# Gate and up chunks 1 to 9 with three seven-product units instead of two, and the low parts of three plain slots made by adding transfers

## What is computed

```python
h = _rmsnorm(x, norm_g)
return (jax.nn.silu(h @ w_gate) * (h @ w_up)) @ w_down      # 2048 -> 5632 -> 2048
```

## Time and profile before

| | |
|---|---|
| runs (median of 3) | 2593.36 us (2592.0 to 2594.75) |
| span of the profiled execution | 2591.4 us, 1.96 us under the median; the profile gives no other time of that execution |
| PE busy | 2562.1 us, 99% |
| DVE, ACT, POOL busy | 1954.8 us (75%), 1339.8 us (52%), 189.2 us (7%) |
| DMA | 548.21 MB, mean 212 GB/s |

### The profile page before, as it was taken

One profiled execution on the slowest core, in us unless ns is written; L12 is line 12 of the kernel. 1 busy time (PEld: TensorE's weight loads), 2 busy tenths in 40 slices (PEclk: granted clock), 3 DMA queues, 4 the chain that ended last, 5 costly groups with the idle time before them and its releaser, 6 DMA issues.

```text
span 2591.4 us, 34224 instructions
## 1 busy us (share of the span) xinstructions
PE 2562.1 (99%) x13659; PEld 2103.4 (81%) x13659; DVE 1954.8 (75%) x2311; ACT 1339.8 (52%) x1568; POOL 189.2 (7%) x346
## 2 busy tenths in 40 slices
PE   8999999999999999999999999999999999999998
PEld 7888888888888777878788888888888888888887
DVE  6888888887767796959666766555668888888876
ACT  5555555555556366446455544433455455555554
POOL 2000000000000011010001112000100000000000
PEclk9999999999999999999999999999999999999999
DMA  6767676667776575656488779643767677766655
GB/s 213 232 210 242 210 236 218 217 208 228 216 210 195 184 228 159 179 165 181 146 280 257 252 245 281 201 155 130 239 190 230 222 226 225 227 219 218 210 201 175
DMA packets 278576, 548.21 MB, mean 212 GB/s; under 512 B 25020, under 2 KB 35424, under 8 KB 278032
## 3 DMA queue, kind: packets, MB, share of 16 engines
q1 hardware_dynamic: 253904, 478.60, 58.3%
q0 software_dynamic: 24192, 66.89, 8.8%
q10 hardware_dynamic: 320, 0.53, 0.1%
HBM read 508.15 MB, written 37.77 MB: 211 GB/s over the span
## 4 chain that ended last, share of the span: by engine, by line
PE 86%; DVE 8%; ACT 3%; DMA 2%; issue 1%; POOL 0%; SPq 0%; DVEq 0%; ACTq 0%; POOLq 0%
PE pp L794 14%; PE pp L795 14%; PE pp L796 14%; PE pp L415 11%; PE pp L416 11%; PE pp L417 11%; DVE wlo L376 2%; PE pa L794 1%; PE pb L796 1%; PE pb L795 1%; PE pb L794 1%; PE pa L795 1%; PE pa L796 1%; ACT whi L371 1%; DMA raw<-in_ffn_w_up 1%
## 5 line engine op out<-in xcount | busy, mean ns | idle before, releaser
L376 DVE TENSOR_TENSOR wlo<-raw,whi 128x1024 fp32r<-128x1024 f32 (+1 forms) x764 | 919.6, 1216 | 345.9 <-ACT whi L371 326.2
L371 ACT ACTIVATE whi<-raw 128x1024 fp32r<-128x1024 f32 (+1 forms) x764 | 798.0, 1053 | 626.5 <-PE pp L417 438.1
L794 PE MATMUL pp<-whi,xhi 128*128 128x512 f32 x1040 | 404.6, 389 | 0.0
L795 PE MATMUL pp<-whi,xlo 128*128 128x512 f32 x1040 | 404.6, 389 | 0.0
L796 PE MATMUL pp<-wlo,xhi 128*128 128x512 f32 x1040 | 404.6, 389 | 0.0
L415 PE MATMUL pp<-whi,xhi 128*128 128x512 f32 (+1 forms) x928 | 370.6, 399 | 0.7 <-DVE xlo L533 0.7
L417 PE MATMUL pp<-wlo,xhi 128*128 128x512 f32 (+1 forms) x928 | 359.6, 388 | 0.1
L416 PE MATMUL pp<-whi,xlo 128*128 128x512 f32 (+1 forms) x928 | 359.6, 387 | 0.0
L847 ACT ACTIVATE whi<-tw 128x1024 fp32r<-128x1024 f32 x124 | 131.6, 1062 | 276.3 <-PE pp L796 131.6
L794 PEld LDWEIGHTS pp<-whi,xhi 128*128 128x128 f32 x1040 | 195.2, 188 | 40.7
L796 PEld LDWEIGHTS pp<-wlo,xhi 128*128 128x128 f32 x1040 | 195.2, 188 | 40.6
(11 more groups left out here) (528 smaller groups left out, 3669.7 us busy)
## 6 DMA issues: line engine op xcount, KB each, us to landing
raw<-in_ffn_w_gate SPq DMA_DIRECT2D x176, 512.0 KB, 4.3
raw<-in_ffn_w_up SPq DMA_DIRECT2D x176, 512.0 KB, 4.7
raw<-in_ffn_w_down SPq DMA_DIRECT2D x176, 512.0 KB, 4.6
raw<-in_w_in SPq DMA_DIRECT2D x144, 512.0 KB, 4.3
hid_dram<-hid_t POOLq DMA_DIRECT2D x43, 512.0 KB, 5.0
xq<-hid_dram POOLq DMA_DIRECT2D x156, 128.0 KB, 3.8
raw<-in_w_lift SPq DMA_DIRECT2D x32, 512.0 KB, 5.9
raw<-in_w_out SPq DMA_DIRECT2D x32, 512.0 KB, 5.1
```

Of the source, the lines that this page charges most:

```text
L371: nc.scalar.activation(whi[:, s, :, 0:width], raw[:, r % RING, :, 0:width], ACT.Copy).then_inc(whi_ready, 1)
L376: nc.vector.tensor_tensor(wlo[:, s, :, 0:width], raw[:, r % RING, :, 0:width], whi[:, s, :, 0:width].bitcast(F32), ALU.subtract).then_inc( ...
L794: nc.tensor.matmul(out, a_hi, whi[:, s, block, :], start=start, stop=False)
L795: nc.tensor.matmul(out, a_lo, whi[:, s, block, :], start=False, stop=False)
```

## The change

Chunks 1 to 9 (`THREE`) of both FFNs get a third unit: slots 5, 6 and 7 of gate and up, after plain slots 1, 3 and 5. With t0 to t9 for the 10 plain slots left, the order is t0 t1 U1 t2 t3 U2 t4 t5 U3 t6 t7 t8 t9. Chunk 10 keeps two units. In chunks 1 to 9 the low parts of t0, t2 and t4 (`LO_ADDED`) no longer come from DVE: ACT writes minus the rounded weights into one of two extra buffers `alo` (`less_hi`), and a transfer issued by POOL adds the weights to it, straight from device memory (`add_raw`). PE reads its low weights there. The SiLU of chunks 1 to 9 moves behind t0 of the next chunk on ACT; `hidden_hi` comes after t8, and `hidden_lo` right behind the gate sum after t9. The forms of the activations for slot 5 are made once per FFN in chunk 0. A few semaphores are merged (`ident_ready` into `consts_ready`, `r_cumx` into `r_cum`, `r_rz` into `r_tilde`), with the same waits in other numbers. Shortened to its core:

```diff
-GU_UNITS, GU_AFTER = (6, 7), (1, 5)
+THREE = range(1, NFC - 1)
+def gu_units(i):
+    return ((5, 6, 7), (1, 3, 5)) if i in THREE else ((6, 7), (1, 5))
+LO_ADDED = (0, 2, 4)
...
+        xs_5 = at("xs_5", AR + 80, [4, P])
+        xshi_5 = at("xshi_5", AR + 36, [4, P], F32R)
+        xslo_5 = at("xslo_5", AR + 38, [4, P], F32R)
+        alo = [at(f"alo{k}", kib, [SK, CW], F32R) for k, kib in enumerate((AR + 32, AR + 76))]
...
+        def wait_lo(eng, n):
+            if n in ADDED:
+                eng.wait_ge(whi_ready, n + 1)
+                eng.wait_ge(sem(f"lo_added{ADDED[n] % 2}"), 16 * (ADDED[n] // 2 + 1))
+            else:
+                eng.wait_ge(wlo_ready, n + 1 - sum(a < n for a in ADDED))
         def raw_free(sp, r):
             if r >= RING:
-                sp.wait_ge(wlo_ready, freed_by[r - RING] + 1)
+                n = freed_by[r - RING]
+                if n in ADDED:
+                    sp.wait_ge(whi_ready, n + 1)
+                    sp.wait_ge(sem("lo_less_hi"), ADDED[n] + 1)
+                else:
+                    wait_lo(sp, n)
...
+        def less_hi(act, n):
+            r, k = raw_of[n], ADDED[n]
+            act.wait_ge(*loaded(r))
+            if k > 1:
+                act.wait_ge(slot_used, list(ADDED)[k - 2] + 1)
+            nc.scalar.activation(alo[k % 2][:, :, :], raw[:, r % RING, :, :], ACT.Copy, scale=-1.0).then_inc(sem("lo_less_hi"), 1)
+        def add_raw(pool, n, w):
+            k = ADDED[n]
+            pool.wait_ge(sem("lo_less_hi"), k + 1)
+            nc.gpsimd.dma_start(alo[k % 2][:, :, :], w.bitcast(F32R),
+                                accum_op=ALU.add).then_inc(sem(f"lo_added{k % 2}"), 16)
...
             for i in range(NFC):
-                hidden_out(pool, tag, i)
+                added = added_of(tag, i + 1)
+                for n, w in added[:2]:
+                    add_raw(pool, n, w)
+                hidden_out(pool, tag, i, lambda: [add_raw(pool, n, w) for n, w in added[2:]])
...
             hi(w + 1, whi[:, (w + 1) % RING, :, :], tw[:, 0:2, :])
+            if ahead is not None:
+                ahead()
...
                 for t, (_, _, w, _) in enumerate(pair["plain"]):
                     split_hi(act, w, 0)
-                    if t in GU_AFTER:
-                        unit_act(act, pair, GU_AFTER.index(t), (tag, "gu", i))
+                    if t == 0 and i - 1 in THREE:
+                        gate_silu(i - 1)
+                    if t in after:
+                        n = after.index(t)
+                        ahead = (lambda: less_hi(act, added[n + 1])) if n + 1 < len(added) else None
+                        unit_act(act, pair, n, (tag, "gu", i), ahead)
...
+                if i + 1 in THREE:
+                    less_hi(act, gu[2 * i + 2]["pair"]["plain"][LO_ADDED[0]][2])
...
                 for t, (_, _, w, _) in enumerate(pair["plain"]):
-                    split_lo(dve, w, 0)
+                    if w not in ADDED:
+                        split_lo(dve, w, 0)
...
-                    if t == pair["na"] + 2:
+                    if t == after[-1] + 3:
                         combine(dve, pair, cb, (tag, "gu", i))
-                    if t == pair["na"] + 3:
+                    if t == after[-1] + 4:
                         combine_last(dve, cb, (tag, "gu", i))
                         v.tensor_tensor(cb[:, 0:2, :], pair_of(gate), cb[:, 0:2, :], ALU.add).then_inc(sem(gate["released"][0]), 1)
+                        if i in THREE:
+                            hidden_lo(dve, tag, i - 1, hhi[:, 4 * i - 4:4 * i, :], hlo[:, 4 * i - 4:4 * i, :])
```

More of the change, by code:

```diff
@@ L737, in x_moved_lo, with added_of @@
             moved_lo(dve, tag, c, xhi[:, 4 * c:4 * c + 4, :], xlo[:, 4 * c:4 * c + 4, :], gain)
+        def added_of(tag, i):
+            weights = A["ffn1_w_gate" if tag == "f1" else "ffn2_w_gate"][0], A["ffn1_w_up" if tag == "f1" else "ffn2_w_up"][0]
+            pair = prods[tag + "gu"][2 * i]["pair"] if i in THREE else None
+            out = []
+            for t in LO_ADDED if i in THREE else ():
+                pr, j, n, _ = pair["plain"][t]
+                w = weights[0 if pr is pair["a"] else 1]
+                out.append((n, w[j * SK * P:(j + 1) * SK * P, i * CW:(i + 1) * CW].rearrange("(k p) n -> p k n", p=P)))
+            return out
         def hidden_turns(pool, tag):
@@ L795, in product @@
             nc.tensor.matmul(out, a_lo, whi[:, s, block, :], start=False, stop=False)
-            return nc.tensor.matmul(out, a_hi, wlo[:, s, block, :], start=False, stop=stop)
+            return nc.tensor.matmul(out, a_hi, (wlo[:, s, :, :] if lo is None else lo)[:, block, :], start=False, stop=stop)
         def plain_pe(pe, pair, t, acts, tts=range(TT), used=1):
@@ L966, in ffn_act, with gate_silu @@
                     forms_hi(act, xs_gu[:, :, :, :], xshi[:, :, :, :], (tag, "x"))
+                    forms_hi(act, xs_5[:, :, :], xshi_5[:, :, :], (tag, "x5"))
+            less_hi(act, gu[2]["pair"]["plain"][LO_ADDED[0]][2])
+            def gate_silu(i):
+                gate = gu[2 * i]
+                act.wait_ge(sem(gate["released"][0]), gate["released"][1])
+                for tt in range(TT):
+                    op = nc.scalar.activation(gs[:, tt, :], cb[:, tt, :], ACT.Silu, scale=rstd[:, tt:tt + 1])
+                op.then_inc(sem("acts_ready"), 1)
@@ L967, in ffn_act @@
             for i in SEVEN:
                 pair = gu[2 * i]["pair"]
-                gate = pair["a"]
+                after = pair["after"]
+                added = [pair["plain"][t][2] for t in LO_ADDED] if i in THREE else []
                 for t, (_, _, w, _) in enumerate(pair["plain"]):
                     split_hi(act, w, 0)
-                    if t in GU_AFTER:
-                        unit_act(act, pair, GU_AFTER.index(t), (tag, "gu", i))
-                    if t == pair["na"]:
+                    if t == 0 and i - 1 in THREE:
[4 more added lines that the diff above has]
+                        unit_act(act, pair, n, (tag, "gu", i), ahead)
+                    if t == after[-1] + 1:
@@ L975, in ffn_act @@
                         act.wait_ge(nat_ready, n0 + i)
                         copy_first(act, pair, cb[:, 0, :])
-                    if t == pair["na"] + 3:
+                    if t == after[-1] + (3 if i in THREE else 4):
+                        if i == NFC - 1:
+                            act.wait_ge(slot_used, pair["units"][-1][1] + UW)
                         hidden_hi(act, tag, i - 1, hhi[:, 4 * i - 4:4 * i, :])
[L979 to L983, removed]
+                    if t == after[-1] + 5:
+                        gate_silu(i)
@@ L2946, in _ @@
         def _(pe):
-            pe.wait_ge(ident_ready, 1)
+            pe.wait_ge(consts_ready, 1)
             gain_turn(pe)
```

98 lines of the change are left out of this document (55 added, 43 removed).

## The result

The changed kernel takes **2753.98 us** (median of 4 runs, 2752.67 to 2761.89) against 2594.06 for the kernel before, run beside it: ratio 1.062, 95% interval 1.0603 to 1.0637. It is slower by 159.9 us, where 49.7 was forecast and 2695 was the range's upper end. The direction and the loop were right; the size was not.

A forecast was written before the change was run, and what follows sets the result against it. PE bound the kernel at 42.16 us a chunk; the change's raw-buffer loop of 43.8 plus 1.3 for transfers gives 45.1. Per FFN 9 x (45.1 - 42.16) - 1.6 = 24.9, twice 49.7: 2643 us, range 2590 to 2695.

The forecast's parts named there:

- the saving: Chunks 1 to 9 of both FFNs: 21 matmuls instead of 24 per added pair, 12.2 us if PE never waits.
- the loop over the two raw places: All units and t8, t9 share two of four raw buffers, so loads wait for third lows: 43.8 us a chunk.
- the bare loop: Rival: adding transfers do not disturb the loads, +26 us, 2620 us; chance 0.25.
- signs named ahead: PE 97 or 98% busy, waiting for `wlo` before unit parts; gate sums 45 us apart; loads issued at the third low ahead.
- So I add 1.3 us a chunk, once: Delay of loads by adding transfers, t4's overlapping U3's pair: 1.3 us a chunk, making the period 45.1.
- its upper bound of 4.7: Most that adding transfers delay a chunk's loads, if each counts double and all three meet a load: 4.7 us.
- POOL's fetches beside other pairs mostly do not show: Argument for undisturbed loads: POOL's fetches mostly show no delay of raw pairs they run beside; no size given.
- t0's meets U1's up load, which has 1.8 us to spare: t0's adding transfer meets U1's up load, whose 1.8 us of slack takes up the delay.
- the add at 5 to 6 us: Each 512 KB adding transfer issued by POOL taken to last 5.0 to 6 us, like POOL's store of that size.
- PE is not in this loop: Chunk's loop of raw buffers runs without PE, which only waits at each unit's last parts.
- heavy transfers: Rival: every add meets a load at double weight, period 47.5 to 48.5, +93 us, 2686 us; chance 0.17.
- Faster: Rival: the loop does not bind, PE stays the bound at 41.48 us a chunk, 2581 us; chance 0.10.

The follow-up runs named there:

- e10: Changed kernel with raw pairs freed at a unit's second low, fetches held until U3's up load landed, all lows on DVE, no adding transfers: 2591.48 us, ratio 0.9967.
- e11: e10 with the turned unit order in gate and up units alone, the down parts' units in the old order: 2588.08 us, ratio 0.9962.
- e5: Changed kernel without adding transfers (some low parts wrong) and with POOL's four fetches held until U3's up load landed: 2622.85 us, +24.5.
- e1: Changed kernel with its 54 adding transfers left out (low parts of t0, t2, t4 wrong), all other waits and the order kept: 2657.95 us, +60.3.
- e3: Changed kernel with POOL's four fetches of hidden values held until U3's up load has landed, adding transfers kept: 2703.21 us, +105.6.
- e7: Changed kernel with raw pairs freed at a unit's second low, late fetches, adding transfers for t0 and t2 only, t4's low on DVE: 2677.73 us, ratio 1.0301.
- e9: Changed kernel with early freed raws, late fetches, `less_hi` one place earlier on ACT, an adding transfer for t2 only: 2620.63 us, ratio 1.0084.
- e2: Changed kernel with plain copies instead of adds in the 54 transfers, so t0, t2 and t4 hold raw weights as low parts: 2709.74 us, +112.1.

## Why the prediction was right or wrong

**Right: the bound before, and the saving.** PE was the bound, and 18 pairs in units save 12.2 us only where PE never waits. e10 and e11 show a chunk of 41.5; they gain 7.5 and 8.8 us by their own medians, not all 12.2. Not every chunk is that short: the mean of e10's sixteen distances is 41.72, against 42.15 in the kernel before, and 18 x 0.43 = 7.7 is about what e10 gains. Why single chunks take up to 42.6 was not tried. The down parts hardly change the sum: in e10 the first FFN's takes 238.2 us instead of 234.0, the second's 231.8 instead of 233.7.

**Right: the loop over the two raw places.** 43.8 us by its rows of the trace of before, 43.87 in the chunk of e5 shown, and +24.5 us where the bare loop was to give +26. (By the mean of 44.05 it would be some +31; the difference is within what single runs differ by, so part of this closeness may be luck.) U1's 7.89, the unit's 5.30 and the way from U3 to the next gate sum held within 0.1 us in both chunks shown. Most signs named ahead came too, though PE's share fell to 95%, not to 97 or 98: PE waits for `wlo` ahead of unit parts (the first of the two largest entries of PE's waits over the run, below), and the loads go out at the third low ahead. DVE's work fitted, as counted.

```profile
PE pa L860 <- DVE wlo L934: 58.8, 41, 3.9
PE pp L860 <- DMA alo<-in_ffn_w_gate: 51.5, 33, 3.9
```

**Wrong: "So I add 1.3 us a chunk, once", and its upper bound of 4.7.** The mean period is 51.41, so the term is 51.41 - 43.8 = 7.6. Some 5.3 of it lie at U3's pair (a mean of 10.5 us to the first sum against 5.2), 1.4 at U1's up load (6.2 against 4.8), 0.9 ahead of U2's first sum, and 0.2 within U1. I priced a load's meeting with *one* transfer, by the distance of two loads that are issued together. At U3's pair three things meet: t4's add, the four fetches and the loads behind the pair. e1 and e3 take one of them away each, and it needs both to bring the pair back to 5.2. The bound was wrong for the same reason: it counted transfers and left out the fetches. Without the fetches it holds: from e5 to e3 the mean distance grows by 48.30 - 44.05 = 4.25.

**Wrong: "POOL's fetches beside other pairs mostly do not show".** I put that down for the bare loop. The unit whose pair the fetches met had slack before; in the loop, each such microsecond is paid. e1 against e5 prices them at 35.8 us. The pair at 291.54, which landed late with those fetches under way, was the row to go by, and I left it out of the sum.

**Wrong in part: "t0's meets U1's up load, which has 1.8 us to spare".** It met it, and used more than that up: DVE waits 2.10 us for it in the chunk shown, and in e1 and e5 the wait is gone (4.72 to the first sum). "t2's is nearly over when U2's pair goes out" held: that pair landed after 4.0 and 4.9 us here, 4.1 and 5.0 in the mean.

**Wrong for t0: the add at 5 to 6 us, and t4's as "the shortest of time".** t4's transfers land after 6.0 us in the median, close to the forecast, and PE waits 19.2 us for them over the run. t0's land after 8.1 (8.4 in the chunk shown), and PE waits 32.3 us for them; the prediction gave t0's transfer no wait of PE at all. In the change most of these 51.5 us lie beside the loop, which is longer: in e3 PE waits 59.1 us for transfers, and the time is 54 us less. But "PE is not in this loop" fails in three of the sixteen chunks: PE's wait for t0's transfer holds back the third high part of U1 on ACT, and U1 takes up to 9.87 us. How much of the waits the end of the kernel sees was not tried alone. In e7 and e9 PE is in the chain, and there they count.

**The rule on adds.** A load of 512 KB takes 54.0% x 2752.3 / 478.6 MB x 0.524 MB = 1.63 us of the 16 DMA engines; an add takes (14.8% x 2752.3 - 8.6% x 2656.2) / 54 = 3.3 us, the 8.6% being the same queue in e1; a plain copy from POOL, worked out the same way from e2, 2.0 us. So an add takes 2.0 times a load, and 1.6 times a plain copy from the same queue. The Trainium skill, in Collectives: The Full Stack, section The bandwidth ceiling, says of a collective's reduce step that its add needs two source reads and so reaches half the rate of a copying step. Against a load these runs agree, against a plain copy from POOL they show less. By that rule alone the forecast would have been 2666, still 88 us short. What the add costs this kernel beyond a plain copy is e2's 47.8 us; the rest is who meets whom.

**The rivals.** The measured time is past heavy transfers (2686), the nearest of them; it has the add at double weight but not the fetches. (Its periods of 47.5 to 48.5 come to 2686 to 2704, so the range's end at 2695 left out half of it, not a third.) The bare loop is what e5 shows, without transfers. Faster needs a shorter loop, and e10 is that.

## What to carry to other kernels

Before a change to an order, list which loads share a place in a small ring, and add up the loop from load to load; a page on which every engine has room says nothing about it. Work moved to DMA was not free here: look at what is issued within some 6 us of each load of the loop (an add took 6.1 to land), small fetches too, and price the meeting of all of them at once, by the bytes that move before the load has landed. Freeing a buffer earlier, by turning two steps of its user, made the third unit pay here, together with later fetches; sparing a busy engine that still met its times did not.

## What the runs showed of the hardware

Transfers in company slow each other far more than the mean share tells: in the chunk shown U3's pair landed 7.3 and 10.8 us after the third low, where e5 has 3.9 and 5.2 in the median, in a stage with a mean DMA share of 0.75. While the pair was under way the share was 1.03, and what grew was the bytes moved in that time, not the time per byte: by the means of sixteen chunks 2.57 MB in 10.4 us, against 1.31 MB in 5.3 us in e5.

A wait of PE can cost more than its length. Timeline and busy times of the changed kernel around PE's wait for t0's transfer (the columns of the windows are those of the earlier trace rows):

```profile
321.67 0.47 PE L860 MATMUL pp<-whi,xhi 128*128 128x512 f32 x1 [2.79 <-DMA alo<-in_ffn_w_gate]
...
322.58 0.63 PE L860 MATMUL pp<-whi,xhi 128*128 128x512 f32 x1
...
323.86 0.63 PE L860 MATMUL pp<-whi,xhi 128*128 128x512 f32 x1
```

```profile
314.50:318.50 4.00, 4.00 (x20) 3.29 (x18) 2.78 (x3) 2.75 (x4) 0.00 (x0) 1.00 0.87 180
321.70:325.50 3.80, 3.80 (x10) 3.04 (x11) 3.80 (x4) 2.00 (x2) 0.54 (x1) 0.57 0.31 119
326.00:328.50 2.50, 2.50 (x13) 2.07 (x12) 2.50 (x4) 0.63 (x1) 0.17 (x1) 1.00 0.54 61
```

Ahead of the wait the granted clock is 1.00. After 2.79 us without work it is 0.57 over the next 3.8 us, that is, mostly at the 1.2 GHz level of its two (1.2 and 2.4), and three matmuls take 1.28 us instead of the 0.68 of the earlier trace rows; then it is 1.00 again. Over the whole run the granted clock is 0.985, in e1 without transfers 0.998; PE's busy time is 2611.8 us, in e1, with the same matmuls, 2581.4. In e7, where PE is in the chain, 12 matmuls behind the 3.58 us wait ran at 0.43 us each instead of 0.2267, at a granted clock of 0.50: 2.4 us more to the 8.41 that ACT waited.
